# Prompt attention on one core: the last block's value matmuls issued ahead of the present block's transposes

## What is computed

```python
def diff_attend(q1, q2, k1, k2, v, q_pos, k_pos, lam):
    s1 = jnp.einsum('nqhd,nkhd->nhqk', q1, k1) * scale + bias
    s2 = jnp.einsum('nqhd,nkhd->nhqk', q2, k2) * scale + bias
    w = jax.nn.softmax(s1, axis=-1) - lam * jax.nn.softmax(s2, axis=-1)
    return jnp.einsum('nhqk,nkhv->nqhv', w.astype(v.dtype), v)
```

## Time and profile before

| | us |
|---|---|
| median of three runs | 1148.66 |
| profiled execution, its own time | 1148.61 |
| its span in the trace | 1146.6 |
| `attend`, first matmul to last matmul in the trace | 290.3 to 392.7 |
| TensorE busy, of the span | 1029.9 |
| VectorE busy | 687.5 |
| ScalarE busy | 527.1 |

### The profile page before, as it was taken

How to read it: one execution, slowest core, us unless ns; L and a number is a source line. 1 busy time by engine, 2 the same in 40 slices (tenths; PEclk the granted TensorE clock), 3 DMA queues, 4 the chain that set the end, 5 groups by cost and what they waited for, 6 DMA issues and landing times. The chain is left out here.

```text
span 1146.6 us, 17847 instructions
## 1 busy us (share of the span) xinstructions
PE 1029.9 (90%) x5490; PEld 846.1 (74%) x5491; DVE 687.5 (60%) x1361; ACT 527.1 (46%) x902; POOL 232.0 (20%) x552
## 2 busy tenths in 40 slices
PE   7999999998899998999982699999999999999920
PEld 6887889787576786688862588888888888888720
DVE  4547557240689625466548656544666698686438
ACT  4232332422588735432212245543555678566334
POOL 0624565800200000000000002221331212223110
PEclk9999999999799999999995799999999999999965
DMA  7130340212850153733320876667869899997355
GB/s 248 51 109 30 86 114 31 68 38 66 293 163 1 48 161 113 298 111 111 121 85 11 325 255 222 195 208 258 290 214 325 269 334 377 354 323 256 111 147 201
DMA packets 52257, 201.34 MB, mean 176 GB/s; under 512 B 10114, under 2 KB 16130, under 8 KB 46050
## 3 DMA queue, kind: packets, MB, share of 16 engines
q1 hardware_dynamic: 41682, 138.43, 34.1%
q0 software_dynamic: 7488, 27.27, 10.1%
q10 hardware_dynamic: 3024, 34.87, 7.8%
HBM read 163.80 MB, written 36.73 MB: 175 GB/s over the span
## 5 line engine op out<-in xcount | busy, mean ns | idle before, releaser
L2135 DVE TENSOR_TENSOR wlo<-raw,whi 128x1024 fp32r<-128x1024 f32 x192 | 221.7, 1219 | 36.5 <-ACT whi L2032 35.7
L2032 ACT ACTIVATE whi<-raw 128x1024 fp32r<-128x1024 f32 x184 | 179.2, 1048 | 30.4 <-PE psG L1977 19.8
L1975 PE MATMUL psG<-whi,exs 128*128 128x512 f32 x200 | 82.0, 410 | 7.1 <-DVE wlo L2135 5.3
L1975 PE MATMUL psY<-whi,ehs 128*128 128x512 f32 x200 | 81.8, 409 | 4.1 <-DVE wlo L2135 4.1
L1940 POOL DMA_INDIRECT acc<-eyb,idxs x25 | 40.8, 1632 | 194.8 <-ACT eyb L2050 194.8
L1976 PE MATMUL psG<-wlo,exs 128*128 128x512 f32 x200 | 79.5, 398 | 0.0
L1977 PE MATMUL psG<-whi,exs 128*128 128x512 f32 x200 | 79.5, 397 | 0.0
L1977 PE MATMUL psY<-whi,ehs 128*128 128x512 f32 x200 | 79.1, 395 | 0.0
L1976 PE MATMUL psY<-wlo,ehs 128*128 128x512 f32 x200 | 78.7, 393 | 0.0
L1975 PE MATMUL psU<-whi,exs 128*128 128x512 f32 x200 | 78.5, 393 | 0.0
L1977 PE MATMUL psU<-whi,exs 128*128 128x512 f32 x200 | 78.4, 392 | 0.0
(11 more groups left out here) (401 smaller groups left out, 2342.6 us busy)
## 6 DMA issues: line engine op xcount, KB each, us to landing
raw<-in_moe_w_gate SPq DMA_DIRECT2D x16, 2048.0 KB, 9.4
raw<-in_moe_w_up SPq DMA_DIRECT2D x16, 2048.0 KB, 9.7
raw<-in_moe_w_down ACTq DMA_DIRECT2D x16, 2048.0 KB, 8.8
w_raw<-in_w_in SPq DMA_DIRECT2D x27, 256.0 KB, 3.4
stg<-in_x_prompt SPq DMA_DIRECT2D x8, 512.0 KB, 4.4
kc<-in_cache_k SPq DMA_DIRECT2D x16, 256.0 KB, 3.0
vc<-in_cache_v SPq DMA_DIRECT2D x16, 256.0 KB, 3.1
mr<-in_w_out SPq DMA_DIRECT2D x8, 512.0 KB, 3.3
```

Of the source, the lines that this page charges most:

```text
L1975: pe.matmul(out, hi, w_hi, start=(k == 0), stop=False)
L2032: nc.scalar.activation(whi[:, at], s.raw[:, at], ACT.Copy).then_inc(hi_made[i], 1)
L2135: nc.vector.tensor_tensor(wlo[:, at], s.raw[:, at], whi[:, at].bitcast(F32), ALU.subtract) \
```

## The change

Two lines in TensorE's order are exchanged: values of n - 1 now stand before turn of n. Nothing is added or removed, and no wait is changed.

```diff
                 for n in range(len(steps)):
                     if n + 2 < len(steps):
                         scores(pe, n + 2)
-                    turn(pe, n)
                     if n >= 1:
                         values(pe, n - 1)
+                    turn(pe, n)
                 values(pe, len(steps) - 1)
```

## The result

| | time, us | ratio to before |
|---|---|---|
| before, 17 runs beside the change | 1147.88 (median) | |
| the change, 17 runs | 1153.99 (median) | 1.0051, 95% interval [1.0038, 1.0063] |
| the change once more, 12 runs | 1153.02 | 1.0034 [1.0018, 1.0050] |
| forecast | 1153.2 (1149.8 to 1156.0) | 1.0040 |

A forecast was written before the change was run, and what follows sets the result against it. It took VectorE to bound the ascents and TensorE the descents of the attend stage. Delays of 3.01 and 1.61 us, together 4.6, on the profiled 1148.61 us gave 1153.2 us, range 1149.8 to 1156.0.

The forecast's parts named there:

- What bounds the stage: In attend, VectorE is the full engine in the ascents, TensorE in the descents, with no gap before the turning.
- The gain at the peaks: At each peak, values fill the 0.21 us gap on TensorE ahead of the turning; the whole gain.
- The mechanism: In the descents, in-order TensorE stands still before a step's values until ScalarE has copied psT to wT.
- the two terms: Delays of the stage: 1.61 us from the first descent into the second ascent, 3.01 us from the second descent.
- the term of 0.10 for a restart: Values starting after a stall cost 0.10 us more per stalled step, 11 steps; bounds 0 and 0.20.
- record + 0.04 + copy + 0.05 + values + 0.10: New turn-to-turn distance in the second descent: 3.75 us at size 7, down to 1.56 at size 2.
- the sum by this alone: If weight loads hide behind running matmuls, nothing of the restart is exposed; the time would be 1152.1 us.
- 11 or 12 waits for the copy of 0.1 to 0.5 us: Sign in the descents: the rows of values get idle time that ScalarE's copy ends.
- The rival of the clock: New stalls at the descents' feet lower TensorE's clock to 1.2 GHz: up to 4.4 us more, 1157.6; chance 0.04.
- a faster kernel: Scores gain on VectorE in the descents and cold start: at most 8.1 us, 1140.5, half 1144.5; chance 0.07.
- The absorbed case: TensorE's stall falls into waits that exist anyway at the descents' feet: 1148.4 to 1150.9 us; chance 0.15.

The follow-up runs named there:

- asc_only: Exchanged order in the ascents only, the order of before in the descents; 0.9996 of before, stage 102.70 us against 102.47.
- change_again: The whole change unaltered, run once more in 12 runs; 1153.02 us, 1.0034 of the kernel before, stage 106.19 us.
- filled_end: The whole change plus three unread score matmuls on TensorE behind the stage's last values; 1.0025 of the kernel before, stage 106.78 us.

## Why the prediction was right, and where not

**What bounds the stage** was read rightly. The ascents cost nothing in asc_only, because VectorE is the full engine there; the descents carry the loss.

**The gain at the peaks** was put at 0.21 us each. At the first peak the scores of the tenth and eleventh step start 4.38 us apart (320.67 and 325.05), where it was 4.56 (318.43 and 322.99); at the second 4.39 (370.18 and 374.57) against 4.56 (366.83 and 371.39). So 0.17 to 0.18: right.

**The mechanism**, values stopped by the copy of their own step, is shown three ways: the new waits of the weight loads (8.4 us, 15 places), the shorter copy (-1.50 us) and the longer one (+2.15, against +0.31 in the old order).

**The size of the two terms** was too large: 4.6 us together, and the trace has 3.27 from the scores of the ninth step on (82.05 against 78.78 us): 1.03 up to the second ascent where I had 1.61, and 2.24 from there where I had 3.01. The step that failed is the term of 0.10 for a restart, in the line record + 0.04 + copy + 0.05 + values + 0.10. Measured from turn to turn the sizes 7 to 2 take 3.60, 3.16, 2.72, 2.29, 1.84 and 1.40 us, 0.14 to 0.16 less than my line each, in 11 steps. 0.10 of this is the restart, which costs nothing. After a stop the first values matmul's record starts with its weight load, at 384.03, and so is 0.10 longer, 1.83 instead of 1.73; but from 384.03 to the next turning at 385.69 it is 1.66, the same as in a running queue. I had read a longer record as a longer stay. The Trainium skill, page "TensorE: Matmul & The Clock Gate", section "Step-by-step: what each phase is for", has the next tile's weights loaded while the present matmul runs, and the sum by this alone was 3.5 us, nearer to the 3.27. The trace agrees with it on the price, that a stop costs nothing beyond itself; it does not show the first load behind a stop as hidden, since load and matmul both stand at 384.03. The other 0.05 are the turning's records, 0.93 at size 7 instead of 0.99, since behind values they too follow in a running queue. A little went the other way: from the scores of size 7 at the second peak to the turn of size 7 the kernel takes 1.76 us longer (11.91 against 10.15), where I had 1.67, and the second ascent is 0.09 us longer, where I had nothing.

**The signs in the profile.** I expected 11 or 12 waits for the copy of 0.1 to 0.5 us. The weight loads have 15, of up to 0.8 us; the matmuls have 8, of up to 0.6 us.

**What the sum did not have.** In the changed kernel's trace the first values matmul, now ahead of the second turning, waited 0.41 us for the load of v. It did so in no other trace of the new order, so it is not a steady cost. The start as a whole scatters by more than that.

**The rival of the clock**, at 0.04, was underrated and in the wrong place. I looked for it at the foot, where the windows still show 1.00. Where it strikes, it does so around the next pause and at the head of the next stage, and costs 1.6 us in four traces and 2.9 in one. My two terms were 1.35 us too large, and a cost behind the stage of about that size, in the executions that have it, was not in the sum. So the forecast of 1153.2 lies within a microsecond of both medians partly by luck: errors that cancel.

**The rivals of no effect and of a faster kernel.** A faster kernel is out. The absorbed case reached up to 1150.9 us, a ratio of 1.0020. The 17 runs exclude it (from 1.0038), and the interval of change_again, from 1.0018, touches its edge alone.

## What to carry to other kernels

On an in-order engine, a wait that vanishes from the profile may only have moved: ask what stands between a producer's work and the engine's own next use of it, and count that distance in time at the smallest size of the loop, not the largest. A round trip through another engine (transposes, copy, matmuls) is hidden by whatever is issued between; moving the last leg forward removes just this cover. And a pause between two stages can cost something behind it too, here 1.6 to 2.9 us in five traces of fourteen behind pauses of about 2 us: look at the granted clock of the first microseconds after each barrier, in more than one execution.

## What was not expected of the hardware

TensorE's granted clock behind the stage is not the same from one execution to the next. It stood at 1.00 or went to 0.50 for some 3 us, once for 7, around a pause of 1.9 to 2.0 us, and with the same old foot it did either. It stayed at 1.00 in all four traces with 0.8 us of work in the pause, behind the old foot or a filled one, and fell in the one trace of filled_end, which had 1.3 us of work in the pause behind the new, thin foot. The late part of the stage, on the other hand, repeats to 0.01 us in five traces of the new order; all the scatter of the stage comes from its first ten steps, where the clock returns.
